# Router logits taken from rows ahead of the first norm, and expert loads issued earlier, in a two-block kernel

## The chip, the cores and the metric

One core of one Trainium2 chip runs the whole program. The metric is the device time of one execution in microseconds (us). The kernel before was run three times.

## The reference

Two transformer-like blocks on 256 tokens of width 1024, all in fp32. The part of the first block that matters here, cut to its core:

```python
merged = sigmoid(gate_a) * y_conv + sigmoid(gate_b) * y_gla
mix = merged @ w_out + b_out
x = layer_norm(ALPHA * x + mix, ln1_g, ln1_b)
ffn = hier_moe(x, w_rg, b_rg, w_re, b_re, w1, w3, w2)
x = layer_norm(ALPHA * x + ffn, ln2_g, ln2_b)
...
def hier_moe(x, ...):
    g_logits = x @ w_rg + b_rg               # 8 groups
    e_all = (x @ w_re + b_re)                # 64 experts, 8 per group
    # one group per token, the two best experts in it, softmax weights
    ...
    hdn = silu(xb @ w1[e]) * (xb @ w3[e])
    out += slot_weight * (hdn @ w2[e])
```

`w1`, `w3` (1024x512) and `w2` (512x1024) of all 64 experts are 403 MB. The second block (four mixers and a gated feed-forward part) follows.

## The kernel before, in words

Every engine has its own program, written out by hand, and they meet through semaphores. `Banks` (L128) hands out the eight PSUM banks in turn; `take` waits until a bank's last reader is done. `Line.done` (L203) makes an engine wait for its own last operation.

**End of the first block's mixers** (`block1_pe`, `block1_dve`, `block1_act`, `block1_sp`). TensorE computes the conv output in eight tiles (`co0` to `co7`, L363). VectorE gates each (`gate_conv`, L971) and adds the other branch into the merged tile (L973), in buffer 8 of `shared`. Then comes the projection: for each half `t` of the 256 rows and each half `s` of the 1024 columns, eight matmuls of 512 columns (L687; each fp32 matmul shows as two instructions). VectorE adds the residual (L1009), takes statistics (L1010, L1015), centres (L1016), inverts the deviation that ScalarE took (L819, L1019) and scales (L1020). Only then does TensorE turn the 128 rows by eight transposes (`turn_rows`, L397, its matmuls at L403), ScalarE copies them out (L826), and TensorE computes the logits (L707, bias L708). `keep_clocked` (L369, L373) is filler work for TensorE.

**The router** (`moe_dve`, from L1397) works on VectorE: the group, the two experts (`chosen`), their weights, their places. Its last reduction is L1437. VectorE then enters its loops and waits for the semaphore `round_moved`, which ScalarE gives. It builds the selection matrices of the first four experts (L1449), TensorE picks rows with them (L1207), and the expert matmuls follow (L1234 for `w1` and `w3`, L1255 for `w2`, L1261 to add up).

**The expert weights** arrive in 96 slabs of 4 MB, six for each group of four experts: two of `w1`, two of `w3`, two of `w2`. There are four slots (`PLACES`, L1106), and slab 1 of the first group goes to four spare buffers in quarters (`load_extra`, L1546). SyncE issues all loads in one order (`moe_sp`, L1519). A load waits for the semaphore `moe_read` of its slot, which TensorE gives when it has read the slab before. The first loads wait for what lay in those buffers: slot 0 is free when the input split is over, slot 1 holds weights of the conv output, slot 2 (`PLACES` 0) holds `w_out`, slot 3 (`PLACES` 6) holds the merged tiles. Once four slots are full, the next load can go only when TensorE has read the first slab.

```python
for i in (2, 3):
    pe.drain().then_inc(S(f"moe_read{i}"), FREED)
...
load(0, 0, 0, True)
for n in (0, 1):
    load_extra(n)
load(2, 0, 0, True)
load_extra(2)
for i in (3, 4):
    load(i, 0, 0, True)
for t in range(TT):
    K.banks1.wait_full(sp, f"logits{t}")
load_extra(3)
```

Of the kernel before, what the change touches and what calls it, by code (L numbers as in the profile page):

```python
# [23 lines left out]
P = 128  # L24
T = 256
TT = T // P
# [39 lines left out]
                 hg_g=2, pool_s=2, n_mem=8, n_mix_pre=8)  # L66
# [330 lines left out]
def turn_rows(K, pe, banks, name, rows, t):  # L397

    for half in range(2):
# [131 lines left out]
def block1_pe(K, pe):  # L531
# [146 lines left out]
    pe.drain().then_inc(S("moe_read1"), FREED)  # L678
    m8 = K.tiles(8, DT)
    for t in range(TT):  # L680
        for s in range(2):
            w = K.slab(R.wait_landed(pe, f"wo{s}"))
            b = B.take(pe, f"wo{t}_{s}")
            for j in range(DT):
                if s == t == 0:
                    pe.wait_ge(S("merged1"), j + 1)
                ins = pe.matmul(K.psum[:, b, :], m8[:, j, t * P:(t + 1) * P], w[:, j, :], start=(j == 0),  # L687
                                stop=(j == DT - 1))
            ins.then_inc(B.full[b], 1)
            if t == TT - 1:  # L690
                R.last_group[f"wo{s}"] = f"wo1_{s}"
    for i in (2, 3):
        pe.drain().then_inc(S(f"moe_read{i}"), FREED)

    V = moe_views(K)
    pe.wait_ge(S("router_in"), 32)
    for t in range(TT):
        if t:
            keep_clocked(K, pe, B, "clocked0", 1)
        pe.wait_ge(S("x1"), t + 1)  # L700
        turn_rows(K, pe, B, "turn_x", K.tiles(1, TT, D), t)
        b = B.take(pe, f"logits{t}")
        o = K.psum[:, b, 0:NG + NE]
        for k in range(DT):
            if k % 4 == 0:
                B.wait_read(pe, f"turn_x{t}_{k // 4}")
            pe.matmul(o, V.x[:, k, t * P:(t + 1) * P], V.w_router[:, k, :], start=(k == 0), stop=False)  # L707
        pe.matmul(o, K.con[32:33, CON["ones"][0]:CON["ones"][0] + P], K.A(5, NG + NE, 1610)[32:33, :], start=False, stop=True)\  # L708
          .then_inc(B.full[b], 1)


def block1_act(K, act):
# [107 lines left out]

    row_sd(0)
    for t in range(TT):
        for half in range(2 - t):
            g = f"turn_x{t}_{half}"
            B.wait_full(act, g)
            L.read(act.activation(x1[:, 4 * half:4 * half + 4, t * P:(t + 1) * P], turned(K, B, "turn_x", t, half),  # L826
                                  ACT.Copy), B, g)
        if t == 0:
            row_sd(1)
        b = B.wait_full(act, f"logits{t}")  # L830
        L.read(act.activation(router_views(K).logits[:, t, :], ps[:, b, 0:NG + NE], ACT.Copy), B, f"logits{t}")
# [3 lines left out]
def block1_dve(K, dve):  # L835
# [124 lines left out]
    ga, gb = K.tiles(8, DT), K.tiles(9, DT)  # L960
# [6 lines left out]
    def gate_conv(m):  # L967
# [5 lines left out]
        L.done(dve.tensor_tensor(ga[:, m, :], ga[:, m, :], gb[:, m, :], ALU.add), S("merged1"))  # L973
# [13 lines left out]
    mem, mem_rstd = K.tiles(10, DT), K.A(5, T, 1756)  # L987
    for m in range(DT):
        gate_conv(m)
        if m == 0:  # L990
# [21 lines left out]
    for t in range(TT):  # L1012
        for s in range(2):
            add_out(t, s)
        L.done(dve.bn_aggr(K.stat("mean_var", 2 * t, 2), K.stat("bn", 12 * t, 12)), S("ln1_stats"))  # L1015
        L.done(dve.scalar_tensor_tensor(x1[:, t, :], x1[:, t, :], K.stat("mean_var", 2 * t), K.gain("ln1_g"),  # L1016
                                        ALU.subtract, ALU.mult), S("dve_steps"))
        dve.wait_ge(S("row_sd"), ROW_SD["ln1"] + t + 1)
        L.done(dve.reciprocal(K.stat("rstd", t), K.stat("sd", t)), S("dve_steps"))  # L1019
        L.done(dve.scalar_tensor_tensor(x1[:, t, :], x1[:, t, :], K.stat("rstd", t), K.gain("ln1_b"),  # L1020
                                        ALU.mult, ALU.add), S("x1"))
    g = f"turn_x{TT - 1}_1"
    B.wait_full(dve, g)
# [82 lines left out]
PLACES = (4, 2, 0, 6)  # L1106
# [75 lines left out]
def moe_pe(K, pe):  # L1182
# [14 lines left out]
    def quad(pair, half, first=False):  # L1197
# [3 lines left out]
        pe.wait_ge(S("total_added"), n * 4 + 1)  # L1201
# [95 lines left out]
def moe_act(K, act):  # L1297
# [10 lines left out]
    L.done(act.activation(K.A(2), K.A(1), ACT.Copy, scale=ALPHA1), S("total_added"))  # L1308
# [23 lines left out]
    act.sem_inc(S("round_moved"), 1)  # L1332
# [10 lines left out]
    act.wait_ge(S("total_added"), rounds * (NQ * 4) + 1)  # L1343
# [19 lines left out]
def router_views(K):  # L1363
    class W:
# [16 lines left out]
        count = K.A(5, 1, 1602)  # L1381
    return W
# [8 lines left out]
def moe_dve(K, dve):  # L1391
# [8 lines left out]
    for t in range(TT):  # L1400
        B.wait_read(dve, f"logits{t}")
# [19 lines left out]
    dve.sem_inc(S("chosen"), 1)  # L1421

# [1358 lines left out]
```

## Time and profile before

| what | value |
|---|---|
| median of 3 runs | 1707.75 us (1706.77 to 1707.82) |
| profiled execution, its own time | 1708.29 us |
| its span | 1706.4 us |
| TensorE busy | 1378.0 us, 81% |
| VectorE busy | 650.5 us, 38% |
| ScalarE busy | 445.5 us, 26% |
| read from HBM | 528.79 MB, 310 GB/s over the span |
| TensorE clock, mean | 0.915 of full |

The span is from the first to the last instruction of the profiled execution. Busy time is not a bound by itself: an engine can be busy while another sets the pace. Times inside the trace are counted from the start of the span.

### The profile page before, as it was taken

To read this page: it belongs to the slowest core of one execution; us is meant where nothing else is said; L and a number is where in the kernel's file an instruction comes from. 1 tells how busy PE (TensorE), PEld (TensorE's weight loads), DVE (VectorE), ACT (ScalarE), POOL (GpSimd) and SP (SyncE) were. 2 spreads that over 40 slices of the span, in tenths; PEclk is the share of its full clock that TensorE was granted. 3 is DMA by queue.
4 is the path that set the end of the run, shared out by engine and by line. 5 is a ranking of instruction groups with operands and counts; after the bars stand their busy time and mean duration, and the time that the engine had idled before them with its cause. 6 is when DMAs were issued, how large, how long until landed. Compare 5 with 4: busy or idle time off the path is not lost.

```text
span 1706.4 us, 20849 instructions
## 1 busy us (share of the span) xinstructions
PE 1378.0 (81%) x8454; PEld 882.1 (52%) x8454; DVE 650.5 (38%) x1076; ACT 445.5 (26%) x645; POOL 0.7 (0%) x6
## 2 busy tenths in 40 slices
PE   8999999877566656666676666566799999999998
PEld 7889986522122212212221222122399989778887
DVE  5887954311011101110110011011266888655874
ACT  4454230201001001000010010010263764456653
POOL 0000000000000000000000000000000000000000
PEclk9999999998788888988887878787899999999999
DMA  8433347799999999999999999999944324565540
GB/s 348 158 136 142 143 157 311 308 425 431 431 429 436 432 432 431 430 431 432 434 432 433 431 430 431 430 433 434 409 180 148 119 80 174 197 240 178 188 173 26
DMA packets 50440, 530.76 MB, mean 311 GB/s; under 512 B 4276, under 2 KB 5556, under 8 KB 33862
## 3 DMA queue, kind: packets, MB, share of 16 engines
q1 hardware_dynamic: 50374, 529.86, 75.0%
q8 instruction: 45, 0.74, 0.2%
q14 instruction: 21, 0.17, 0.0%
HBM read 528.79 MB, written 1.05 MB: 310 GB/s over the span
## 4 chain that ended last, share of the span: by engine, by line
PE 55%; DMA 40%; DVE 2%; ACT 1%; issue 1%; SPq 0%; DVEq 0%; ACTq 0%
DMA ring<-in_w 35%; PE psum L363 9%; PE psum L445 6%; PE psum L446 6%; PE psum L447 6%; PE psum L1234 5%; PE psum L1987 4%; PE psum L1255 4%; DMA shared<-in_w 4%; PE psum L1988 2%; PE psum L1261 2%; PE psum L687 2%; PE psum L1207 1%; PE psum L1824 1%; DMA arena<-in_w 1%; PE psum L549 1%
## 5 line engine op out<-in xcount | busy, mean ns | idle before, releaser
L1234 PE MATMUL psum<-shared,arena 128*32 128x512 f32 x1008 | 148.1, 737 | 78.5 <-DMA shared<-in_w 78.4
L1234 PE MATMUL psum<-ring,arena 128*32 128x512 f32 x1024 | 144.1, 716 | 69.9 <-DMA ring<-in_w 69.8
L1464 DVE TENSOR_TENSOR shared<-shared,psum 128x512 f32<-128x512 f32 x16 | 11.0, 686 | 461.6 <-PE psum L1234 461.6
L1234 PEld LDWEIGHTS psum<-shared,arena 128*32 128x32 f32 x1008 | 35.5, 131 | 181.4 <-DMA shared<-in_w 96.1
L445 PE MATMUL psum<-parts 128*128 128x256 f32 (+1 forms) x392 | 128.0, 327 | 0.0
L1255 PE MATMUL psum<-ring,shared 128*32 128x512 f32 x512 | 81.6, 784 | 56.8 <-DMA ring<-in_w 56.8
L447 PE MATMUL psum<-parts 128*128 128x256 f32 (+1 forms) x392 | 126.8, 323 | 0.0
L446 PE MATMUL psum<-parts 128*128 128x256 f32 (+1 forms) x392 | 126.7, 323 | 0.0
L1255 PE MATMUL psum<-shared 128*32 128x512 f32 x512 | 81.6, 784 | 53.4 <-DMA shared<-in_w 52.7
L1234 PEld LDWEIGHTS psum<-ring,arena 128*32 128x32 f32 x1024 | 35.9, 128 | 171.3 <-issue 91.4
L1987 PE MATMUL psum<-parts 128*128 128x512 f32 x308 | 110.5, 398 | 1.3 <-DVEq L2545 1.3
L1466 DVE COPY shared<-psum 128x512 f32<-128x512 f32 x16 | 11.1, 691 | 249.8 <-PE psum L1255 249.8
L1713 DVE TENSOR_TENSOR parts<-ring,parts 128x1024 fp32r<-128x1024 f32 x66 | 80.9, 1225 | 56.4 <-ACT parts L1706 54.1
L864 DVE SCALAR_TENSOR_TENSOR arena<-arena,vec 128x256 f32<-128x256 f32 x240 | 98.7, 479 | 2.0
L445 PE MATMUL psum<-parts,ring_parts 128*128 128x256 f32 x336 | 96.0, 286 | 1.3 <-DVE ring_parts L1661 0.7
L446 PE MATMUL psum<-rowbuf_parts,ring_parts 128*128 128x256 f32 x336 | 94.6, 282 | 0.0
L447 PE MATMUL psum<-parts,ring_parts 128*128 128x256 f32 x336 | 93.9, 279 | 0.0
L1988 PE MATMUL psum<-parts 128*128 128x256 f32 x352 | 91.6, 281 | 0.0
L1706 ACT ACTIVATE parts<-ring 128x1024 fp32r<-128x1024 f32 x66 | 70.0, 1061 | 74.0 <-PE psum L1989 41.1
L1326 ACT ACTIVATE arena<-psum 128x256 f32<-128x256 f32 x16 | 6.1, 383 | 316.9 <-PE psum L1244 316.9
L1207 PE MATMUL psum<-arena 128*128 128x128 f32 x512 | 65.2, 288 | 27.4 <-DVE arena L1449 27.4
L1330 ACT ACTIVATE shared<-psum 128x512 f32<-128x512 f32 x16 | 9.6, 597 | 295.0 <-PE psum L1255 295.0
(304 smaller groups left out, 2264.1 us busy)
## 6 DMA issues: line engine op xcount, KB each, us to landing
shared<-in_w SPq DMA_DIRECT2D x47, 4096.0 KB, 32.3
ring<-in_w SPq DMA_DIRECT2D x47, 4096.0 KB, 32.5
ring<-in_w_in SPq DMA_DIRECT2D x19, 2048.0 KB, 8.5
ring<-in_w_ffn_gate_up SPq DMA_DIRECT2D x11, 2048.0 KB, 8.5
ring<-in_w_gate SPq DMA_DIRECT2D x8, 2048.0 KB, 7.8
ring<-in_w_ffn_down SPq DMA_DIRECT2D x5, 2048.0 KB, 7.7
ring<-in_w_out SPq DMA_DIRECT2D x4, 2048.0 KB, 7.6
ring<-in_w_gla_out SPq DMA_DIRECT2D x2, 2048.0 KB, 7.6
```

The lines of the kernel that those rows point to most:

```text
L363: m = pe.matmul(o, weights[k], acts[k], start=(k == 0), stop=(k == n - 1 and bias is None))
L445: pe.matmul(out, w[0], x[0], start=start, stop=False)
L446: pe.matmul(out, w[0], x[1], start=False, stop=False)
L447: return pe.matmul(out, w[1], x[0], start=False, stop=stop)
L864: ins = dve.scalar_tensor_tensor(conv[:, m, :], u[:, m, w:w + T], cw[:, m, w:w + 1], conv[:, m, :], ALU.mult, ALU.add)
L1207: m = pe.matmul(ps[:, bank, k % 4 * P:(k % 4 + 1) * P], V.x_rows[:, t, k * P:(k + 1) * P], V.sel[:, t, :], start=(t == 0), stop=(t == TT - 1))
L1234: m = pe.matmul(ps[slots, bank, :], V.picked[:, k, slots], w[e * len(w) // QUAD][:, e % (QUAD // len(w)), j, :], start=(k == 0), stop=(k = ...
L1255: m = pe.matmul(ps[slots, MOE_BANK["down"][c], :], V.hidden_t[:, f, slots], w(e), start=(f == 0), stop=(f == ET - 1))
L1706: L.done(L.eng.activation(self.shaped(n, 0), src, ACT.Copy), K.sem("unit_high"))
L1713: L.done(L.eng.tensor_tensor(self.shaped(n, 1), src, self.shaped(n, 0).bitcast(F32), ALU.subtract), K.sem("unit_low"))
L1987: pe.matmul(ps[:, b, :], w[0][:, k, :], sp.both[:, k, :, :], start=(k == 0), stop=False)
L1988: m = pe.matmul(ps[:, b, 0:T], w[1][:, k, :], sp.u[0][:, k, :], start=False, stop=False)
```

## The change

It moves and adds work, and computes the same thing.

The logits are taken from the rows before the norm. With x the row before the norm, m its mean and r its inverse deviation, the logits of the normed row are r (x @ (g w)) - r m (sum of g w) + (sum of b w + bias). So VectorE scales the router's weights by the gain and takes two column sums (`router_sums`) while the conv output is computed. TensorE spreads them over the partitions by two small matmuls (`router_const`), and turns the rows before the norm and computes their logits between the matmuls of the projection. VectorE scales and shifts the result (`logit_shift`, `logits`). The scaling of the second 128 rows stands in the router, behind `chosen`.

The merged tiles go to buffer 2, which the total of the experts uses later. ScalarE writes that total when both halves of the rows are ready, under a semaphore `total_ready` of its own. VectorE gives `round_moved` itself for the first round. Slots 2 and 3 change places (`PLACES`), the slot of the merged tiles being free when they have been added. Load 0 and the quarters 0 and 1 go behind `co0`, load 3 behind the last merged tile.

```diff
+def ps_cols(K, b, n):
+    return K.psum[:, b, 0:n]
@@ block1_pe
-    pe.drain().then_inc(S("moe_read1"), FREED)
-    m8 = K.tiles(8, DT)
-    for t in range(TT):
-        for s in range(2):
...
-    for i in (2, 3):
-        pe.drain().then_inc(S(f"moe_read{i}"), FREED)
...
+    for i in (1, 2):
+        pe.drain().then_inc(S(f"moe_read{i}"), FREED)
+    W = router_views(K)
+    ones_row = K.con[32:33, CON["ones"][0]:CON["ones"][0] + P]
+    pe.wait_ge(S("router_sums"), 2)
+    b = B.take(pe, "router_const")
+    pe.matmul(ps_cols(K, b, 2 * (NG + NE)), K.c("ones"), W.column_sums, start=True, stop=False)
...
+    def turn(t, half):
+        B.wait_read(pe, f"wo{t}_{half}")
+        turn_rows(K, pe, B, "turn_x", rows, t, (half,))
+    def logits(t, half):
+        group = f"logits{t}"
+        b = B.place[group][0] if half else B.take(pe, group)
+        B.wait_read(pe, f"turn_x{t}_{half}")
+        for k in range(4 * half, 4 * half + 4):
+            m = pe.matmul(ps_cols(K, b, NG + NE), V.x[:, k, t * P:(t + 1) * P], V.w_router[:, k, :], start=(k == 0),
+                          stop=(k == DT - 1))
+        if half:
+            m.then_inc(B.full[b], 1)
+    project(0, 0)
+    project(0, 1)
+    turn(0, 0)
+    project(1, 0)
+    turn(0, 1)
+    project(1, 1, 0, 4)
+    turn(1, 0)
+    logits(0, 0)
+    logits(0, 1)
+    project(1, 1, 4, DT)
+    pe.drain().then_inc(S("moe_read3"), FREED)
+    logits(1, 0)
+    turn(1, 1)
+    logits(1, 1)
@@ block1_dve
+    def router_sums(name, scaled, out):
+        gain = last(K.v(name, 0, DT), NG + NE)
+        L.done(dve.tensor_tensor(scaled, V.w_router, gain, ALU.mult), S("dve_steps"))
+        L.done(dve.tensor_reduce(out, scaled.rearrange("p k n -> p n k"), AX, ALU.add), S("router_sums"))
...
+    add_out(0, 0)
+    add_out(0, 1)
+    gathered(0)
+    logit_shift(0)
+    add_out(1, 0)
+    centred(0)
+    scaled_rows(K, L, 0)
+    logits(0)
+    add_out(1, 1)
+    gathered(1)
+    centred(1)
+    logit_shift(1)
+    logits(1)
@@ block1_sp
-    for slab in SLABS1[-4:]:
+    load("co0")
+    moe_load(K, sp, 0, 0, 0, True)
+    for n in (0, 1):
+        moe_load_extra(K, sp, n)
+    for slab in ("co1", "wo0"):
         load(slab)
...
+    load("wo1")
@@
-PLACES = (4, 2, 0, 6)
+PLACES = (4, 2, 6, 0)
@@ moe_act
-    L.done(act.activation(K.A(2), K.A(1), ACT.Copy, scale=ALPHA1), S("total_added"))
+    act.wait_ge(S("x1"), TT)
+    L.done(act.activation(K.A(2), K.A(1), ACT.Copy, scale=ALPHA1), S("total_ready"))
...
-    act.sem_inc(S("round_moved"), 1)
@@ moe_dve
     dve.sem_inc(S("chosen"), 1)
+    scaled_rows(K, L, 1)
...
+        dve.wait_ge(S("total_ready"), 1)
...
+    dve.sem_inc(S("round_moved"), 1)
@@ moe_sp
-    load(0, 0, 0, True)
-    for n in (0, 1):
-        load_extra(n)
     load(2, 0, 0, True)
-    load_extra(2)
+    moe_load_extra(K, sp, 2)
+    sp.wait_ge(S("merged1"), DT)
     for i in (3, 4):
         load(i, 0, 0, True)
```

SyncE, from the first load of the conv output's weights to the last load ahead of the experts' loop, before (`in_w` is the experts' weights, `bank_full` a finished PSUM group; the name in front of `<-` is the buffer written):

```order
L1057 DMA ring<-in_w_conv_out 128x4096 [waits bank_full2]
L1057 DMA ring<-in_w_conv_out 128x4096 [waits bank_full6]
...
L1057 DMA ring<-in_w_out 128x4096 [waits bank_full0]
L1074 DMA arena<-in_x_rows 128x2x1024 [waits bank_full6]
L323 DMA arena<-in_gains 128x1024 [waits conv_act]
...
L1537 DMA shared<-in_w 128x8192 [waits moe_read0]
L1549 DMA rowbuf<-in_w 128x2048
L1549 DMA shared<-in_w 128x2048
L1537 DMA ring<-in_w 128x8192 [waits moe_read1]
...
L1537 DMA ring<-in_w 128x8192 [waits moe_read2]
L1537 DMA shared<-in_w 128x8192 [waits moe_read3]
L1549 DMA arena<-in_w 128x2048 [waits bank_full4,bank_full0]
```

And the same stretch of SyncE in the changed kernel:

```order
L1130 DMA ring<-in_w_conv_out 128x4096 [waits bank_full2]
L1615 DMA shared<-in_w 128x8192 [waits moe_read0]
L1628 DMA rowbuf<-in_w 128x2048
L1628 DMA shared<-in_w 128x2048
L1130 DMA ring<-in_w_conv_out 128x4096 [waits bank_full6]
...
L1130 DMA ring<-in_w_out 128x4096 [waits bank_full0]
...
L1615 DMA ring<-in_w 128x8192 [waits moe_read1]
L1628 DMA shared<-in_w 128x2048
L1615 DMA shared<-in_w 128x8192 [waits merged1,moe_read2]
L1615 DMA ring<-in_w 128x8192 [waits moe_read3]
L1628 DMA arena<-in_w 128x2048 [waits bank_full3,bank_full2]
```

The load into slot 0 and two quarters moved ahead of the second slab of the conv output's weights. The load into slot 2 now waits for the last merged tile instead of the end of the projection.

TensorE, from the last two groups of the projection to the logits, before:

```order
L687 MATMUL psum<-ring,shared 128x512 [waits bank_free5,ring1_landed1]
L687 MATMUL psum<-ring,shared 128x512 x7
L403 MATMUL psum<-con,arena 128x128 [waits bank_free6,x1,router_in]
L403 MATMUL psum<-con,arena 128x128 x3
L403 MATMUL psum<-con,arena 128x128 [waits bank_free7]
...
L707 MATMUL psum<-shared,arena 128x72 [waits bank_free6,bank_free0]
L707 MATMUL psum<-shared,arena 128x72 x3
...
L708 MATMUL psum<-shared,con 128x72
```

And in the changed kernel, from the first half of the last group (L703 is the projection, L408 the turn, L719 the logits):

```order
L703 MATMUL psum<-ring,arena 128x512 [waits bank_free0,ring1_landed1]
L703 MATMUL psum<-ring,arena 128x512 x3
L408 MATMUL psum<-con,arena 128x128 [waits bank_free1,bank_free6]
...
L719 MATMUL psum<-shared,arena 128x72 [waits bank_free5,bank_free2]
...
L719 MATMUL psum<-shared,arena 128x72 [waits bank_free7]
...
L703 MATMUL psum<-ring,arena 128x512 [waits ring1_landed1]
L703 MATMUL psum<-ring,arena 128x512 x3
L719 MATMUL psum<-shared,arena 128x72 [waits bank_free1,bank_free3]
...
L408 MATMUL psum<-con,arena 128x128 [waits bank_free4,bank_free0]
...
L719 MATMUL psum<-shared,arena 128x72 [waits bank_free4]
```

Before, the turns and logits stand behind the whole projection and wait for the normed rows (`x1`). Now three of the four turns and the first logits stand within it, and only half a turn and the second logits behind it.

VectorE, in the router, from `chosen` to the start of its loops, in the changed kernel:

```order
L1481 TENSOR_SCALAR shared<-shared 128x128 [waits dve_steps]
L1096 SCALAR_TENSOR_TENSOR arena<-arena,stats 128x1024 [waits dve_steps]
L1479 TENSOR_TENSOR shared<-shared 128x128 [waits expert_exp,x1]
...
L1520 TENSOR_REDUCE shared<-psum 128x1 [waits bank_full0,bank_free7]
L1559 UNCONDITIONAL_BRANCH [waits bank_free0]
L1560 UNCONDITIONAL_BRANCH
L1560 ISA
L1532 ISA [waits round_moved]
L1532 TENSOR_TENSOR arena<-con,shared 128x128
```

The row at L1096, the scaling of 128 rows of 1024, is new in this place; the rest stands as before.

## Rows read from the trace of the kernel before

**Rows 1.** The page: chain by line, and GB/s in 40 equal slices.

```profile
DMA ring<-in_w 35%; PE psum L363 9%; PE psum L445 6%; PE psum L446 6%; PE psum L447 6%; PE psum L1234 5%; PE psum L1987 4%; PE psum L1255 4%; DMA shared<-in_w 4%; PE psum L1988 2%; PE psum L1261 2%; PE psum L687 2%; PE psum L1207 1%; PE psum L1824 1%; DMA arena<-in_w 1%; PE psum L549 1%
...
GB/s 348 158 136 142 143 157 311 308 425 431 431 429 436 432 432 431 430 431 432 434 432 433 431 430 431 430 433 434 409 180 148 119 80 174 197 240 178 188 173 26
```

**Rows 2.** Windows: length, PE, PEld, DVE, ACT, POOL busy, clock, DMA share, GB/s.

```profile
292.00:307.00 15.00, 15.00 (x36) 6.46 (x34) 5.71 (x8) 0.29 (x1) 0.00 (x0) 1.00 0.08 34
...
331.00:332.00 1.00, 0.77 (x7) 0.58 (x6) 0.00 (x0) 0.20 (x1) 0.00 (x0) 1.00 0.12 49
...
346.00:1210.00 864.00, 564.89 (x3570) 192.13 (x3570) 87.01 (x165) 59.83 (x90) 0.00 (x0) 0.84 1.00 431
```

**Rows 3.** Timeline of SyncE's queue: start, length, line, operation, count.

```profile
252.18 0.40 SPq L1537 DMA_DIRECT2D shared<-in_w  x1
...
279.53 0.33 SPq L1537 DMA_DIRECT2D ring<-in_w  x1
...
307.50 0.33 SPq L1537 DMA_DIRECT2D ring<-in_w  x1
...
331.07 0.35 SPq L1537 DMA_DIRECT2D shared<-in_w  x1
341.06 3.80 SPq L1537 DMA_DIRECT2D ring<-in_w  x2
```

**Rows 4.** Timeline of TensorE, 279 to 334 us: start, busy, line, idle before.

```profile
279.65 27.70 PE L687 MATMUL psum<-ring,shared 128*128 128x512 f32 x64 [0.26 <-issue]
307.73 1.07 PE L403 MATMUL psum<-con,arena 128*128 128x128 f32 x8 [0.38 <-issue]
309.20 1.98 PE L707 MATMUL psum<-shared,arena 128*128 128x72 f32 x16 [0.40 <-ACT arena L826]
311.11 0.44 PE L708 MATMUL psum<-shared,con 1*128 1x72 f32 x2
...
324.19 2.92 PE L1207 MATMUL psum<-arena 128*128 128x128 f32 x24 [2.31 <-DVE arena L1449]
327.04 3.64 PE L1234 MATMUL psum<-shared,arena 128*32 128x512 f32 x32
...
333.39 0.59 PE L1234 MATMUL psum<-rowbuf,arena 128*32 128x512 f32 x1 [1.62 <-DMA arena<-in_w]
```

**Rows 5.** Timeline of VectorE and ScalarE, 306 to 326 us.

```profile
310.69 1.28 DVE L1020 SCALAR_TENSOR_TENSOR arena<-arena,stats 128x1024 f32<-128x1024 f32 x1
...
313.16 0.60 ACT L826 ACTIVATE arena<-psum 128x512 f32<-128x512 f32 x1 [1.29 <-PE psum L403]
...
316.70 0.17 DVE L1398 TENSOR_REDUCE shared<-shared 128x2 f32<-128x16 f32 x1 [2.41 <-ACT shared L831]
...
319.96 0.23 DVE L1397 TENSOR_SCALAR shared<-shared 128x128 f32<-128x128 f32 x1
...
322.23 0.22 DVE L1437 TENSOR_REDUCE shared<-psum 128x1 f32<-128x64 f32 x1
...
323.44 0.49 DVE L1449 TENSOR_TENSOR arena<-con,shared 128x128 f32<-128x128 f32 x2 [0.99 <-ACTq L1332]
```

**Rows 6.** Chain that ended last, in order of time: start, length, what.

```profile
185.91 93.48 PE psum L363 x432
...
316.32 16.93 DMA arena<-in_w
```

**Rows 7.** Groups of VectorE, 255 to 281 us: busy, mean ns, idle before.

```profile
L971 DVE SCALAR_TENSOR_TENSOR shared<-psum,vec,shared 128x256 f32<-128x256 f32 x8 | 3.9, 483 | 16.3 <-PE psum L363 16.3
```

**Rows 8.** DMA issues from 279 to 280 us: KB, us from issue to landing.

```profile
ring<-in_w SPq DMA_DIRECT2D x1, 4096.0 KB, 11.9
```

**Rows 9.** DMA issues from 331 to 332 us.

```profile
shared<-in_w SPq DMA_DIRECT2D x1, 4096.0 KB, 15.3
```

**Rows 10.** DMA queues from 345 to 520 us: packets, MB, share of 16 engines.

```profile
q8 instruction: 6, 0.10, 0.2%
```

**Rows 11.** Timeline of TensorE, 1190 to 1213 us.

```profile
1202.09 5.34 PE L1234 MATMUL psum<-shared,arena 128*32 128x512 f32 x32 [4.08 <-DMA shared<-in_w]
```

More of the change, by code:

```diff
@@ L394, in pe_mean_by_tile, with turn_rows @@
     m.then_inc(banks.full[b], 1)
-def turn_rows(K, pe, banks, name, rows, t):
-    for half in range(2):
+def turn_rows(K, pe, banks, name, rows, t, halves=(0, 1)):
+    for half in halves:
         b = banks.take(pe, f"{name}{t}_{half}")
@@ new lines, in block1_pe, with project @@
+    W = router_views(K)
[3 more added lines that the diff above has]
+    pe.matmul(ps_cols(K, b, 2 * (NG + NE)), K.c("ones"), W.column_sums, start=True, stop=False)
+    pe.matmul(K.psum[:, b, NG + NE:2 * (NG + NE)], ones_row, K.A(5, NG + NE, 1610)[32:33, :], start=False, stop=True)\
+      .then_inc(B.full[b], 1)
+    m8, V, rows = K.tiles(2, DT), moe_views(K), K.tiles(1, TT, D)
+    def project(t, s, k0=0, k1=DT):
+        w = K.slab(R.wait_landed(pe, f"wo{s}"))
+        group = f"wo{t}_{s}"
+        b = B.take(pe, group) if k0 == 0 else B.place[group][0]
+        for j in range(k0, k1):
+            if s == t == 0:
+                pe.wait_ge(S("merged1"), j + 1)
+            ins = pe.matmul(K.psum[:, b, :], m8[:, j, t * P:(t + 1) * P], w[:, j, :], start=(j == 0), stop=(j == DT - 1))
+        if k1 == DT:
+            ins.then_inc(B.full[b], 1)
+        R.last_group[f"wo{s}"] = group
@@ L819, in row_sd, with turned_rows @@
         L.done(act.activation(K.stat("sd", t), K.stat("mean_var", 2 * t + 1), ACT.Sqrt, bias=K.c("ln_eps")), S("row_sd"))
+    def turned_rows(t, half):
+        g = f"turn_x{t}_{half}"
+        B.wait_full(act, g)
+        L.read(act.activation(x1[:, 4 * half:4 * half + 4, t * P:(t + 1) * P], turned(K, B, "turn_x", t, half), ACT.Copy),
+               B, g)
     row_sd(0)
     for t in range(TT):
[L823 to L831, printed above, removed]
+        for half in range(2):
+            turned_rows(t, half)
+    row_sd(1)
     act.preload_act_table(ACT.Exp)
@@ L1200, in quad @@
         pe.wait_ge(S("sel_built"), n * 4 + 2)
-        pe.wait_ge(S("total_added"), n * 4 + 1)
+        if first and half == 0:
+            pe.wait_ge(S("x1"), TT)
+        else:
+            pe.wait_ge(S("total_added"), n * 4)
         def pick(a, b):
@@ new lines, in moe_load @@
+def moe_load(K, sp, i, first, pair, start=False, final=False):
+    S, d, ring = K.sem, K.d, MoeRing(K)
+    t = ring.turn(i, start)
+    i %= PAIR * len(SLABS3)
+    name, cut = SLABS3[i % len(SLABS3)]
+    sp.wait_ge(ring.passed(t), pair * USES + t // RSLABS + FREED)
+    sp.sem_inc(S("set_wanted"), 1)
+    dst = ring.slab(t, 1).rearrange("p e k n -> p k (e n)")
+    src = d[name].rearrange("s p n -> p s n")[:, bass.ds(first + (i // len(SLABS3) * CUTS + cut), 1), :]
+    if not final:
+        sp.dma_start(dst, src).then_inc(ring.landed(t), 16)
+        if (name, cut) == SLABS3[-1]:
+            for piece in (1, 2, 3):
+                sp.sem_inc(S(f"w2_piece{piece}"), 16)
+        return
+    for piece in range(4):
+        h = slice(SLAB_COLS // 4 * piece, SLAB_COLS // 4 * piece + SLAB_COLS // 4)
+        sp.dma_start(dst[:, :, h], src[:, :, h]).then_inc(S(f"w2_piece{piece}") if piece else ring.landed(t), 16)
@@ L1560, in moe_sp @@
         K.banks1.wait_full(sp, f"logits{t}")
[L1561 removed]
+    moe_load_extra(K, sp, 3)
     sp.wait_ge(S("rounds_known"), 1)
@@ L2319, in inverse_sums @@
             B.wait_read(dve, f"{name}{AH - 1}")
-        L.done(dve.reciprocal(V.sums, V.sums), S("sums"))
+        L.done(dve.reciprocal(V.sums, V.sums), step)
     def shares(name):
```

108 lines of the change are left out of this document (41 added, 67 removed).

## The prediction

> **What bounds the kernel now.** I read the page first: the row of bytes per slice and the chain of waits [rows 1]. From slice 9 to slice 28 the core moves 430 GB/s without a break, and 35% of the chain that ended last is the expert weights landing in `ring`. The windows say the same of one stretch: from 346 to 1210 us the 16 DMA engines are at share 1.00 and 431 GB/s, with TensorE busy 565 of 864 us [rows 2]. That is 9.7 us for a 4 MB slab (4.194 MB / 431 GB/s). There are 96 slabs, so the middle of the kernel is one stream, and its end is where it starts plus its length. No instruction of the change alters the bytes. So the question is what sets the start of the stream, and whether all of its bytes must be moved after that.
>
> Next the queue of SyncE [rows 3]. I call the loads #0, #2, #3, #4 (4 MB each) and e0 to e3 (the quarters of slab 1). Before, #0 and e0, e1 go at 252 us, #2 with e2 at 279.5, #3 and #4 at 307.5, e3 at 316.3 [rows 6] and #5 at 331.07. From 292 to 307 the DMA engines stand at share 0.08, so 15 us are idle there; from 331 to 332 they stand at 0.12 [rows 2]. Then #5 starts the stream. #5 goes into the slot of #0 and is issued when TensorE has read #0: its 32 matmuls run from 327.04 for 3.64 us, to 330.7 [rows 4]. Whatever is loaded earlier, #5 waits for this. **The start of the stream hangs on the chain projection, norm, router, first selection, first slab, and not on the loads before it.**
>
> Third, that chain [rows 4, 5]. The projection runs 279.65 to 307.35. The router's first operation on VectorE is at 316.70, 9.35 us later. Its last reduction ends at 322.45, VectorE then waits 0.99 us for a semaphore of ScalarE, the selection starts at 323.44, the first pick at 324.19, the first slab at 327.04.
>
> **The change, part by part.** *#0, e0 and e1 go at 200 us instead of 252.* They are 6.3 MB, 14.6 us at 431 GB/s. Behind them on SyncE stand `co1`, `wo0`, the rows of x, `wo1` and two gains. `co1` waits for its slot until about 214 anyway, and is read only in the second half of the conv output, which runs to 279.4. TensorE runs one unbroken piece from 185.9 to 279.4 [rows 6], so nothing there waits for a load. Cost nothing. If that cover went, each load would be late by at most 14.6 us less its slack of tens of us.
>
> *Column sums on VectorE.* Four operations on 576 elements at the second and third tile of the conv output. The trace has none of this size; the nearest are 1.28 us for 1024 columns [rows 5] and 0.48 for 256 [rows 7], so they cost 2 to 5.1 us together. I take 2.8, by size. The eight operations at L971 waited 16.3 us in all for TensorE [rows 7], and the two gaps used are about 2 us each. Hidden. If it were not, the last merged tile would be late, and the projection asks for that one only at its eighth matmul.
>
> *TensorE gets work before the end of the projection.* The constant: one matmul of 144 columns and one on one partition, at most 0.44 us for such a pair [rows 4], 0.6 together. Three turns of 4 transposes, half of the 1.07 us that 8 take [rows 4]: 1.6. The logits of the first 128 rows: 1.9 (16 instructions from 309.20 to 311.11) [rows 4]. Sum 4.1, all on the path, since the projection is unbroken. It ends at 307.35 + 4.1 = 311.45.
>
> *The chain behind it is shorter.* Before 9.35 us. Now: 0.38 until TensorE starts again (307.35 to 307.73), 0.95 for half of the logits, 0.53 for the last turn, 0.2 to ScalarE, 0.60 for its copy [rows 5], 0.14, 0.95 for the other half, then 0.1 and 0.24 for the scaled sum on VectorE: 4.1. Beside it VectorE has the centring (1.28), a reciprocal and two small operations behind the last turn, which ends about 0.15 later; I take 4.25. The router starts at 315.7, 1.0 us earlier.
>
> *Behind the router.* One 1024-column operation (1.28, with its gap 1.32) [rows 5] now stands between `chosen` (320.19) and the weights, ahead of everything that leads to the selection: 1.32 later. The wait of 0.99 us for ScalarE goes, since VectorE now gives that semaphore itself. What takes its place is VectorE's own way into its loop, which the trace hides under that wait: between 0 and 0.99, I take 0.5, the middle. Net: 1.0 - 1.32 + 0.99 - 0.5 = 0.2 us earlier for the selection, for the first slab and for #5. The bounds are 0.7 earlier and 0.3 later, and 1 us more on either side for the inserted TensorE work.
>
> *#3 goes at 280.5 and #4 at about 312.* #2, e2 and #3 are 9.4 MB, done by 304; #4 and e3 are done by about 326 instead of 333.25 (316.32 + 16.93, the end of e3 in the chain) [rows 6]. So the idle stretch moves: it was 292 to 307, now it is some 8 us before 312 and some 6 us from 326 to 332. The 4 MB brought forward do not shorten the stream, because #5 is not ready to follow. This is why a load moved by 27 us is worth almost nothing by itself.
>
> *What a queue that has run empty is worth.* TensorE waited 1.62 us for e3 [rows 4]; that goes, and #6 (issued at 341.06) [rows 3] goes about 1 us earlier. #5 needed about 1 us from issue to its bytes (331.07 to 332) and 9.7 us of transfer, so it left the engines at 341.7 while #6 could start at 342.1: 0.4 us regained. By mean bytes the sum is therefore 0.2 + 0.4 = 0.6 us. But a slab counts when its last part has landed. #2, issued into an empty queue, landed after 11.9 us [rows 8]. #5, issued behind e3, landed after 15.3 [rows 9]. Some of the 16 engines were behind by 3.4 us, and at a constant pace this lag stays to the end of the stream. After the change #5 finds the queue empty, as #2 did: 0.2 + 3.4 = 3.6 us.
>
> The Trainium skill, DMA: Bandwidth & Descriptors, section Why a DMA increments its semaphore by 16 and not by 1, says that a transfer runs "on up to 16 SDMA engines that finish independently, and the semaphore counts them". By that rule the sum would be 3.6, by the mean bytes of the windows 0.6; the 15.3 beside 11.9 us agrees with the rule.
>
> Between 0.6 and 3.6 I choose by the instruction packets. From 345 to 520 us six of them take 0.2% of 16 engines [rows 10], 0.2% x 16 x 175 / 6 = 0.9 us of one engine each. An engine hit twice is 1.9 us behind, and becomes the new slowest one: 3.6 - 1.9 = 1.7 us. Behind the stream nothing changes. The profiled execution took 1708.29 us (span 1706.4), so it should take 1706.6. The median of the runs, 1707.75, is 0.5 below it: **forecast 1706.0**, from 1707.75 - 1.7 = 1706.05.
>
> **The rivals.** What can be told from no change is 0.2%, 3.4 us.
> A. The forecast, 1706.0, chance 0.52.
> B. No gain from the lag: instruction packets or the start-up leave one engine as late as before, or the inserted work costs 1 us more. Gain 0.6 down to a loss of 1.3: 1707.2 to 1709.1. For it speaks that six such packets fall into the 175 us behind the start of the stream [rows 10]. Chance 0.28.
> C. The lag goes entirely and the chain is at its best bound: 3.4 + 0.7 = 4.1, 1703.6. Against it: the packets. Chance 0.12.
> D. The 9.7 us of #3 come off the whole: 1698.0. For it: 15 idle us of DMA. Against it: #5 waits for the read of #0. Only if the first slab could be read 9 us sooner. Chance 0.03.
> E. Slower: TensorE's clock. Before, TensorE stood idle 2.31 us before the first pick and kept full speed (32 matmuls in 3.64) [rows 4]. After an idle 4.08 us late in the stream the same 32 took 5.34 [rows 11]. Now its filler work ends earlier and the selection hardly does, so the idle is about 2.8 us. If the clock falls to its lower level (1.2 of 2.4 GHz), the pick (2.92) and the slab (3.64) double, #5 goes 6.5 us later, and with the 1.7 gained the time is 1707.75 + 4.8 = 1712.5. It decides somewhere between 2.31 and 4.08 us of idle. Chance 0.05.
>
> The Trainium skill, TensorE: Matmul & The Clock Gate, section Part 1: The HAM clock gate, says that "the default state is throttled, and activity releases the throttle"; the 5.34 beside 3.64 us agrees, and it is the rule by which E would come.
>
> **How the numbers follow.** The likeliest case gives 1706.0. The range, 1703.6 to 1709.2, takes in A, B and most of C, and leaves out D, E and the far edge of C, about 1 in 10. Faster by over 0.2%: C and D, 0.15. Slower: E, 0.05. Within: 0.80.
>
> **What would show each step.** #5 issued between 330.0 and 331.5 us. The projection's last matmul at 311 to 312. The DMA share near zero for some us just before #5, and full from there to about 1208. #5 landing 11.9 to 13 us after its issue. The first TensorE wait for e3 gone. No wait of VectorE between 185 and 280 that holds TensorE. I am wrong if #5 goes more than 1.5 us away from 331, if TensorE's granted clock is below 1.00 between 320 and 335, or if the stream's length from #5 to its end changes by more than 3.6 us.

## The result, and the profile after

| | before | after |
|---|---|---|
| median | 1707.37 us (1705.91 to 1708.74, 15 runs) | 1710.03 us (1707.96 to 1712.07, 15 runs) |
| profiled execution, its own time | 1708.29 | 1710.75 |
| its span | 1706.4 | 1709.0 |

The ratio is 1.0014, 95% interval 1.0008 to 1.0021: the change made the kernel 0.14% slower, 2.7 us. That is less than the 0.2% that I called the bound of what can be told, but the interval excludes no change, and 1710.0 is outside my range of 1703.6 to 1709.2. The spans differ by 2.6 us, so the two traces hold the loss. Of all executions of this document one was slow: one of the eleven of `b_vec16` (experiment 1) took 1898.59 us at a mean granted clock of 0.72, and the ratios leave it out.

**Up to the first pick the trace does what I said.** SyncE after, its last loads:

```profile
200.34 0.35 SPq L1615 DMA_DIRECT2D shared<-in_w  x1
...
280.41 0.33 SPq L1615 DMA_DIRECT2D shared<-in_w  x1
311.41 0.33 SPq L1615 DMA_DIRECT2D ring<-in_w  x1
315.02 0.33 SPq L1628 DMA_DIRECT2D arena<-in_w  x1
333.25 0.35 SPq L1615 DMA_DIRECT2D shared<-in_w  x1
```

VectorE after:

```profile
315.61 0.17 DVE L1482 TENSOR_REDUCE shared<-shared 128x2 f32<-128x16 f32 x1
...
319.27 1.28 DVE L1096 SCALAR_TENSOR_TENSOR arena<-arena,stats 128x1024 f32<-128x1024 f32 x1 [0.15 <-DVE shared L1481]
...
322.48 0.22 DVE L1520 TENSOR_REDUCE shared<-psum 128x1 f32<-128x64 f32 x1
323.28 0.49 DVE L1532 TENSOR_TENSOR arena<-con,shared 128x128 f32<-128x128 f32 x2 [0.58 <-DVEq L1558]
```

The projection's last piece starts at 307.63 and lasts 3.65, so it ends at 311.28 (forecast 311.45). The router starts at 315.61 (315.7), and the selection at 323.28: 0.16 us earlier than in [rows 5], where I had worked out 0.2. VectorE's way into its loop took 0.58, where I took 0.5. The four operations for the column sums took 3.9 us together, where I took 2.8, and no wait of TensorE between 185 and 280 us answers to them.

**The first pick.** TensorE after, the rows that answer to [rows 4]:

```profile
307.63 3.65 PE L703 MATMUL psum<-ring,arena 128*128 128x512 f32 x8
...
324.03 5.26 PE L1288 MATMUL psum<-arena 128*128 128x128 f32 x24 [3.47 <-DVE arena L1532]
329.21 3.64 PE L1315 MATMUL psum<-shared,arena 128*32 128x512 f32 x32
...
334.63 0.62 PE L1315 MATMUL psum<-rowbuf,arena 128*32 128x512 f32 x1 [0.69 <-ACT arena L1400]
```

The 24 matmuls of the pick took 5.26 us instead of 2.92 [rows 4], after an idle 3.47 instead of 2.31. The windows say why (from 320 to 327 us; the columns are those of [rows 2]). Before:

```profile
320.00:327.00 7.00, 4.43 (x36) 3.95 (x34) 3.74 (x14) 3.38 (x4) 0.49 (x2) 1.00 1.02 437
```

After:

```profile
320.00:327.00 7.00, 3.53 (x19) 3.42 (x19) 3.41 (x13) 3.49 (x4) 0.49 (x2) 0.65 0.72 305
```

The granted clock fell from 1.00 to 0.65, a mean over both of its levels: it was 1.00 up to 321 us, 0.69 from 321 to 324, so it fell while TensorE was still idle, and 0.50 from 324 to 328. The slab behind the pick ran its 3.64 us at full speed again. So the fall cost 2.34 us, and #5 went 2.18 us later than in [rows 3], at 333.25. The wait for `e3` of 1.62 us [rows 4] is gone, as predicted.

**The stream took that back.** Windows after:

```profile
292.00:307.00 15.00, 15.00 (x53) 7.79 (x51) 6.22 (x10) 2.09 (x4) 0.00 (x0) 1.00 0.74 316
308.00:331.00 23.00, 18.14 (x100) 13.56 (x102) 11.74 (x40) 7.16 (x13) 0.49 (x2) 0.85 0.57 229
331.00:332.00 1.00, 1.00 (x16) 0.35 (x12) 0.00 (x0) 0.00 (x0) 0.00 (x0) 1.00 0.00 0
346.00:1210.00 864.00, 561.95 (x3574) 189.07 (x3574) 87.36 (x166) 60.39 (x91) 0.00 (x0) 0.85 1.00 432
```

The idle stretch of the DMA engines has moved from 292 to 307 us [rows 2] to the time before #5, and #5 finds its queue empty (DMA share 0.00 from 331 to 332). DMA issues after, the row of #5, from 333 to 334 us:

```profile
shared<-in_w SPq DMA_DIRECT2D x1, 4096.0 KB, 13.5
```

It landed after 13.5 us, not 15.3 [rows 9]. To measure the stream I take a mark in the second block that every build has, 64 matmuls in 13.81 us (I call it the mark). It stands first in each of the next two fences.

**The loss is behind the stream.** The chain of waits in order of time: start, length, what. Before:

```profile
1242.36 13.81 PE psum L1747 x64
1273.13 1.78 PE psum L1787 x16
1286.22 1.78 PE psum L1787 x16
...
1380.92 2.03 PE psum L1902 x24
```

After:

```profile
1241.86 13.81 PE psum L1830 x64
1272.94 1.79 PE psum L1870 x16
1286.24 1.79 PE psum L1870 x16
...
1382.13 2.03 PE psum L1985 x24
```

From #5's issue to the mark it was 911.29 us before (1242.36 - 331.07), and is 908.61 now: 2.68 shorter. So the mark is 0.50 earlier (1241.86 against 1242.36). From the mark to the end of the span it was 464.04 (1706.4 - 1242.36), and is 467.14: 3.10 longer, in a part of the program that the change does not touch. This adds up: -0.16 (selection) + 2.34 (clock) - 2.68 (stream) + 3.10 = 2.6.

What is longer there? Between the mark's end and the first row of 16 stand 144 matmuls of `three_passes`. They took 1273.13 - 1256.17 = 16.96 us before, 117.8 ns each, and 1272.94 - 1255.67 = 17.27 now, 119.9 ns each. One in three of them, the second of each triple, reads `rowbuf_parts`. Groups of TensorE from 1255 us to the end, before:

```profile
L445 PE MATMUL psum<-parts,ring_parts 128*128 128x256 f32 x336 | 96.0, 286 | 1.3 <-DVE ring_parts L1661 0.7 <-ACT shared L2021 0.6
L446 PE MATMUL psum<-rowbuf_parts,ring_parts 128*128 128x256 f32 x336 | 94.6, 282 | 0.0
L447 PE MATMUL psum<-parts,ring_parts 128*128 128x256 f32 x336 | 93.9, 279 | 0.0
```

After:

```profile
L450 PE MATMUL psum<-parts,ring_parts 128*128 128x256 f32 x336 | 97.2, 289 | 0.7 <-DVE ring_parts L1744 0.4 <-ACT shared L2104 0.2
L451 PE MATMUL psum<-rowbuf_parts,ring_parts 128*128 128x256 f32 x336 | 95.4, 284 | 0.0
L452 PE MATMUL psum<-parts,ring_parts 128*128 128x256 f32 x336 | 95.4, 284 | 0.0
```

Some 1000 such matmuls at 2.1 ns more make about 2.1 us. The rest is one place. The chain after, at 1378 us:

```profile
1378.02 0.58 PE psum L450
1378.60 0.22 PE psum L451
1378.82 0.21 PE psum L452
...
1380.32 0.15 PE psum L450
1380.46 0.12 PE psum L451
```

Most of the matmuls there stand at 0.21 us instead of 0.12. The ten from 1378.02 on take 2.44 us to the end of the tenth; before, the same ten took 1.45 (1377.83 to 1379.28). Windows before and after, the same stretch:

```profile
1377.80:1380.30 2.50, 2.47 (x21) 2.48 (x21) 1.06 (x1) 2.34 (x6) 0.00 (x0) 1.00 0.00 0
```

```profile
1377.80:1380.30 2.50, 2.30 (x12) 2.28 (x11) 1.23 (x2) 2.34 (x6) 0.00 (x0) 0.51 0.00 0
```

The granted clock is 0.51 there, about its lower level (1.2 of 2.4 GHz). It costs 1.0 us, and 2.1 + 1.0 makes the 3.10.

### The profile page after: what moved, and what is told of

Same layout as the page of the kernel before. It is cut to its first block, busy times and chain, and to the rows that moved or that the text cites. A ratio compares the mean times of both kernels' runs of the same rounds, so it can differ in the third digit from the quotient of the medians.

```text
span 1709.0 us, 20845 instructions
## 1 busy us (share of the span) xinstructions
PE 1378.2 (81%) x8452; PEld 883.3 (52%) x8452; DVE 656.0 (38%) x1086; ACT 445.8 (26%) x644; POOL 0.7 (0%) x6
## 4 chain that ended last, share of the span: by engine, by line
PE 57%; DMA 38%; DVE 3%; ACT 1%; issue 1%; DVEq 0%; SPq 0%; ACTq 0%
DMA shared<-in_w 37%; PE psum L363 9%; PE psum L450 6%; PE psum L1315 6%; PE psum L451 6%; PE psum L452 6%; PE psum L2070 4%; PE psum L1336 4%; PE psum L2071 2%; PE psum L1342 2%; PE psum L1288 2%; PE psum L703 2%; PE psum L1907 1%; PE psum L554 1%; PE psum L2041 1%
## 5 line engine op out<-in xcount | busy, mean ns | idle before, releaser
L1336 PE MATMUL psum<-shared 128*32 128x512 f32 x512 | 89.4, 834 | 68.5 <-DMA shared<-in_w 68.5
L1336 PE MATMUL psum<-ring,shared 128*32 128x512 f32 x512 | 75.5, 743 | 44.3 <-DMA ring<-in_w 43.6
```

Source lines behind the costliest of these rows:

```text
L1336: m = pe.matmul(ps[slots, MOE_BANK["down"][c], :], V.hidden_t[:, f, slots], w(e), start=(f == 0), stop=(f == ET - 1))
```

## The experiments

My theories after the traces. **Place:** the change adds sixteen columns (eight of gain and eight of bias of the first norm) to the constant buffer `vec`, 64 bytes per partition, and every buffer declared behind it moves by 64 bytes; `rowbuf_parts` is one, and the matmuls of `three_passes`, which work with it, became slower. **Clock:** the longer idle before the first pick costs 2.3 us. Rivals: the second block is slower in some executions whatever the place; the early loads themselves are what costs.

The experiments ran in three jobs; the kernel before ran in each (medians 1707.6, 1707.05, 1707.94 us).

**1. `b_vec16`: the kernel before, with the 16 columns and nothing else.**

```diff
-                 hg_g=2, pool_s=2, n_mem=8, n_mix_pre=8)
+                 hg_g=2, pool_s=2, n_mem=8, n_mix_pre=8, ln1_gain=8, ln1_shift=8)
```

> The kernel before, with the 16 further columns in the vector table and nothing else; they push the buffer `rowbuf` (read as `rowbuf_parts` by the three-pass matmuls of the second block) 64 bytes further. Theory of the address: those 1056 matmuls go from 117.8 to about 120 ns each, so the time rises by 2.0 to 3.1 us over before, all of it between 1255 and 1490 us of the span. Rival, the loss comes from the moved router and loads: no change within 0.7 us.

1708.89 us, ratio 1.0008 (0.9999 to 1.0017). From the mark to the end 466.10 us (before 464.04), 144 matmuls in 17.28. So the slower pace comes with the columns, without any other part of the change. The whole, 1.3 us above the kernel before of its job, is less than the 2.0 to 3.1 that I expected, and its interval just reaches no change: the stream was shorter here, to which "Read together" below returns.

**2. `a_tail`: the changed kernel, the 16 columns in a buffer of their own behind all others.**

```diff
-        self.vec = sb("vec", NVEC)
+        self.vec = sb("vec", NVEC - TAIL)
...
+        self.vec_tail = sb("vec_tail", TAIL)
```

> The changed kernel, with its 16 columns in a small buffer behind all others, so that every other buffer lies where it lay before. Theory of the address: 2.0 to 3.1 us less than the changed kernel, so about 1707.3, equal to before; the second block is back at its old length. Rival: no different from the changed kernel, 1710.0. Either way the first pick is still slow (24 matmuls in 5.3 us), since the addresses do not touch it.

1707.84 us, ratio 1.0004 (0.9995 to 1.0013). This removes 2.2 us of the loss (1710.03 - 1707.84), as expected. From the mark to the end it is 464.29, 2.85 less than in the changed kernel: the 144 matmuls are back at 16.96 us, and the fall of the clock at 1378 us is also absent from this trace (granted clock 1.00 from 1373 to 1381).

**3. `a_clk`: the changed kernel, six more filler matmuls before the first pick.**

```diff
+    for _ in range(6):
+        pe.matmul(ps[:, 5, 0:T], K.c("ident"), K.con[:, CON["after"][0]:CON["after"][0] + T], start=True, stop=True)
     for g in ("before0", "before1", "chose"):
```

> The changed kernel with six filler matmuls on TensorE behind the three router matmuls, so that it idles about 0.8 us before the first pick instead of 3.47. Theory of the clock: the pick takes 2.92 instead of 5.26 us, load 5 is issued about 2.3 us sooner (331.0), and the whole kernel is 2.0 to 2.3 us shorter than the changed one, 1707.8. Rival, the stream hides it (the stretch behind load 5 gave it back): less than 0.7 us.

1708.27 us, ratio 1.0005 (0.9996 to 1.0014): 1.8 below the changed kernel, a little less than the 2.0 to 2.3 that I expected. Timeline of TensorE, the pick:

```profile
324.71 2.92 PE L1290 MATMUL psum<-arena 128*128 128x128 f32 x24 [0.83 <-DVE arena L1534]
```

It is back at 2.92 us, and it waits for the selection (L1534) as before, not for the fillers, which end at 323.89. It starts 0.7 later than in the changed kernel only because the projection already started that much later in this execution (281.15 against 280.44). #5 went at 331.59, 1.66 earlier than in the changed kernel, and the mark came 1.69 earlier.

**4. `a_tail_clk`: both edits.**

> Both edits together. If address and clock add up: 4.3 to 5.4 us less than the changed kernel, 1705.2, which is 2.2 us less than before. If they overlap: about 1707.5.

1706.35 us, ratio 0.9994 (0.9985 to 1.0003), 3.7 below the changed kernel. The two effects about add up (2.2 + 1.8 = 4.0), though it is less than the 4.3 to 5.4 that I expected. One thing in its timeline of TensorE is not as in the other builds:

```profile
312.65 1.25 PE L723 MATMUL psum<-shared,arena 128*128 128x72 f32 x8 [0.75 <-ACT arena L856]
313.69 5.68 PE L382 MATMUL psum<-con 128*128 128x256 f32 x18
```

These 18 filler matmuls took 4.10 us in the changed kernel; the granted clock is 0.50 from 314 to 316 us here, after an idle of only 0.75. They push the new fillers past the selection, so the pick starts without an idle, at 323.42, about 0.6 later than it could (selection at 322.10, and 0.75 from there to the pick in the changed kernel).

**5. `a_tail_clk_late`: the same, with load 3 held until the projection has ended**, so that loads 3 and 4 both go at 312 us.

```diff
-    sp.wait_ge(S("merged1"), DT)
+    sp.wait_ge(S("moe_read3"), FREED)
     for i in (3, 4):
```

> The kernel with both edits (columns at the end, six filler matmuls), and load 3 held back until the projection is read, so that loads 3 and 4 go together at 311 us as they did at 307.5 before. Theory of the empty queue: the queue is still busy with e3 when load 5 is issued, load 5 lands 15 us and not 13.6 us after its issue, and the kernel is 1 to 2 us slower than with load 3 at 280 us. Rival: the preloads never matter, no difference within 0.5 us.

1712.56 us, ratio 1.0031 (1.0021 to 1.0042): 6.2 above `a_tail_clk` (of another job; 6.3 by the two ratios), much more than the 1 to 2 that I expected. Its timeline shows a chain that I had not seen. SyncE:

```profile
311.67 0.33 SPq L1622 DMA_DIRECT2D shared<-in_w  x1
312.11 0.36 SPq L1622 DMA_DIRECT2D ring<-in_w  x1
315.24 0.33 SPq L1635 DMA_DIRECT2D arena<-in_w  x1
331.12 0.35 SPq L1622 DMA_DIRECT2D shared<-in_w  x1
347.97 0.34 SPq L1622 DMA_DIRECT2D ring<-in_w  x1
```

TensorE:

```profile
337.60 1.03 PE L1322 MATMUL psum<-rowbuf,arena 128*32 128x512 f32 x1 [5.79 <-DMA arena<-in_w]
```

The quarter `e3` lands behind loads 3 and 4. TensorE waits 5.79 us for it, reads slab 1 late, and #6 goes at 347.97 instead of 339.29; the engines run dry (DMA share 0.65 from 340 to 350 us, where `a_tail_clk` has 0.98). The changed order of the projection delays load 4 from 307.5 to 311.4, and the early load 3 is what pays for that.

**6. `b_clk`: the kernel before, four more filler matmuls** (the edit of 3, at the same place).

> The kernel before, with four filler matmuls (1.9 us) behind the three router matmuls, so that TensorE idles about 0.4 us and not 2.31 before the first pick. In the profile of the kernel before the clock held there, in that of the one with 16 more columns it did not, after the same idle. If the clock falls in part of the executions of before: 0.3 to 1.2 us less than before, 1706.8. If it nearly never does: no change, 1707.6. The distance to the kernel with both edits says what moving the router and the loads is worth by itself: 0 to 1.5 us.

1707.73 us, ratio 1.0002 (0.9993 to 1.0011): no gain. The pick took 2.92 us after an idle 0.54, as in the kernel before after 2.31, so there was nothing to win at the pick. In its trace the mark comes 1.65 us earlier than before (1240.71), but the clock falls behind it (0.50 from 1375 to 1377 us), and from the mark to the end it is 465.29, 1.25 longer. Against `a_tail_clk`, by the two ratios, the router and the loads are worth 1.4 us, in the range of 0 to 1.5 that I gave; the intervals overlap.

**7 to 11. Where the place matters.** Unused columns in the kernel before, each one execution with a profile, so that the times of single pieces in the trace can be compared and the whole time can't.

```diff
         self.vec = sb("vec", NVEC)
+        self.pad = sb("pad", 8)
```

`b_pad32` and `b_pad256` have 32 and 256 columns at the same place. `b_pad16_row` has 16 directly ahead of `rowbuf`, so that only `rowbuf` and the statistics behind it move. `b_pad16_end` has 16 behind `rowbuf`, so that only the statistics move.

> The kernel before with `rowbuf` 32 bytes further on, and nothing else. Look at the three-pass matmuls at L445 to L447 from 1256 us on: before one came every 117.8 ns, with 64 bytes more every 120. If what counts is the place within 64 bytes, some third value, up to 120; if only half-way steps of 128 bytes count, 117.8 as before.

> The kernel before with `rowbuf` 128 bytes further on. If the pace repeats every 128 bytes: 117.8 ns a matmul and the second block as long as before. If any shift costs: 120 ns and 2 us more.

> The kernel before, with 64 unused bytes per partition right ahead of rowbuf, so that the vector constants, wf and small stay where they were and rowbuf (with the small statistics behind it) alone is shifted. If the place of rowbuf sets the matmuls' pace: the second block is 1.5 to 3 us longer than before, the matmuls that read rowbuf_parts at 284 to 290 ns instead of 279 to 286. Rival (the shift of wf, small or the constants does it): second block within 0.5 us of before.

> The kernel before, with 64 unused bytes per partition behind rowbuf: only the statistics and two counters are shifted. If the place of rowbuf sets the pace: the second block is within 0.5 us of before, matmuls at 279 to 286 ns. Rival (statistics): 1.5 to 3 us longer.

> The kernel before, with 1024 unused bytes per partition behind the vector constants. If the pace goes by the place of rowbuf modulo some power of two up to 1024 bytes: second block within 0.5 us of before. If the place before is favourable by its distance to another buffer or by larger blocks: 0.9 to 3 us longer, as after 32, 64 and 128 bytes.

| build | `rowbuf` moved by | 144 matmuls | mark to end | the execution |
|---|---|---|---|---|
| before | 0 | 16.96 | 464.04 | 1708.29 |
| `b_pad16_end` | 0 | 16.96 | 464.23 | 1707.86 |
| `b_pad8` | 32 bytes | 17.08 | 465.00 | 1709.46 |
| `b_pad16_row` | 64 bytes | 17.27 | 466.03 | 1710.82 |
| `b_vec16` | 64 bytes | 17.28 | 466.10 | 1708.34 |
| `b_pad32` | 128 bytes | 17.26 | 465.68 | 1709.05 |
| `b_pad256` | 1024 bytes | 16.96 | 464.41 | 1707.17 |

The chain of `b_pad16_row`:

```profile
1242.97 13.81 PE psum L1748 x64
1274.05 1.79 PE psum L1788 x16
1287.35 1.79 PE psum L1788 x16
```

The place of `rowbuf` alone sets the pace; what stands ahead of it or behind it does not matter. The rival that the second block is slower in some executions whatever the place is out: over all fourteen profiled builds the 144 matmuls take 16.96 us in the eight with `rowbuf` at its old place or 1024 bytes further, 17.26 to 17.28 in the five with 64 or 128 bytes, and 17.08 in the one with 32. That 1024 bytes bring the old pace back fits a rule that goes by the place within blocks of at most 1024 bytes; one build at one such distance does not show the rule. `b_pad32` has the pace of 64 bytes in the 144 matmuls but is 0.3 to 0.4 us shorter than those two from the mark to the end; that is not explained.

Why the place matters stays open. By the starts in the chain, the steps behind the first, second and third matmul of a triple take 120, 118 and 115 ns on average before, and 120 each after. They are 120 each in all five builds with 64 or 128 bytes. In the eight at the old pace some steps are shorter, and not the same ones: the third in `a_tail_clk` (113), the first in `a_tail_clk_late` (116). So what is lost is now and then a shorter step, and it is not tied to the one matmul of the three that reads the moved buffer.

**12. `a_tail_clk_l0`: as `a_tail_clk`, load 0 and the quarters 0 and 1 at their old place** (252 us instead of 200).

```diff
     load("co0")
-    moe_load(K, sp, 0, 0, 0, True)
-    for n in (0, 1):
-        moe_load_extra(K, sp, n)
```

> The changed kernel with the constants at the end and the six filler matmuls, as a_tail_clk, but load 0 and the quarters 0 and 1 issued where they stood before, behind the gains, at about 252 us instead of 200. My reasoning said that their place is worth nothing, since load 3 at 280 is what the early loads give: 1706.3, within 1 us of a_tail_clk, #5 at 330 to 331. Rival (the three loads push load 2, 3 and the quarter 2 later, so that these land beside the projection's end and the stream starts with uneven engines): #5 lands 15 to 16 us after its issue, 1708 to 1712.

1705.88 us, ratio 0.9990 (0.9981 to 0.9999), #5 at 330.11, landing 13.6 us later. Moving these three loads earlier gives nothing. This build has the lowest median of all, 2.1 us below the kernel before of its job, and is the only one whose interval excludes no change on the faster side, by 0.01%. So neither the early load 3 (experiment 5) nor these three are what costs.

**Read together: the stream and the clock.** Timeline and DMA issues of all fourteen builds:

| builds | idle, pick | #5 issued | lands after | #5 to the mark |
|---|---|---|---|---|
| before, `b_pad8`, `b_pad32`, `b_pad16_row`, `b_pad16_end` | 2.3, 2.92 | 330.8 to 331.7 | 13.9 to 15.3 | 910.9 to 911.4 |
| `b_clk` | 0.54, 2.92 | 330.92 | 14.8 | 909.8 |
| `b_vec16`, `b_pad256` | 2.3, 4.54 and 4.14 | 332.06, 332.53 | 13.6, 13.5 | 908.3, 908.4 |
| after, `a_tail` | 3.47, 5.26 and 5.13 | 333.25, 332.03 | 13.5, 13.6 | 908.6, 909.1 |
| `a_clk`, `a_tail_clk`, `a_tail_clk_l0` | 0.8 (none in `a_tail_clk`), 2.8 to 2.9 | 330.1 to 331.6 | 13.6 | 908.3 to 908.6 |
| `a_tail_clk_late` | 0.82, 2.92 | 331.12 | 16.1 | 915.4 |

Two things are seen. Wherever #5 landed within 13.6 us of its issue, the stretch to the mark was 908.3 to 909.1; where it was issued behind an `e3` that was still arriving, it was 1 to 3 us longer. The first kind also has an earlier #6: 9.05 to 9.07 us after #5 in those seven builds, 9.75 to 10.03 in the six behind `e3`, where TensorE waits 1.40 to 1.67 us for `e3`. The empty queue and the earlier #6 always came together, so these runs do not tell which of them shortens the stream. And in two builds of the kernel before the clock fell after an idle of only 2.3 us. It delayed #5 by a good microsecond, but cost nothing: the later #5 found an empty queue, and the mark was no later (1240.40 and 1240.89, before 1242.36). In its trace this is why `b_vec16` lost less than its slower pace: from #5 to the mark it is 2.95 us shorter than before, with #5 only 0.99 later. In the changed kernel the queue is empty anyway, so the fall costs its price (the 1.69 at the mark in `a_clk`).

## Why the prediction was wrong, point by point

**The step that failed** is the sentence "Behind the stream nothing changes." It rests on the order of instructions, which indeed does not change there. The term that I put at nothing measured 3.10 us (467.14 against 464.04). Sixteen new columns in a constant buffer move `rowbuf` by 64 bytes, and the matmuls of `three_passes` then start every 119.9 instead of 117.8 ns: 2.1 us. My diff left these columns out, and no rival speaks of addresses. Experiments 1, 2 and 7 to 11 show this cause. The other 1.0 us behind the stream is the clock at 1378 us. Such a fall, somewhere from 1371 to 1385 us, is in six of the fourteen profiled builds, in after and in all five with more fillers, and not in before. In all six the stretch from the mark to the end is about 1 us longer than in the builds with the same pace and no fall (465.06 to 465.29 against 464.04 to 464.41; 466.93 and 467.14 against 466.03 and 466.10). I have no cause for it: after an idle of 2.05 us (before), 1.95 (`b_vec16`) and 1.95 (after) the clock held in the first two and fell in the third. It stays open, and with it whether this term belongs to the change at all.

**Rival E, to which I gave 0.05, happened in its first half.** The idle was 3.47 us, not my 2.8, and the clock fell. I had doubled the pick and the slab, 6.5 us; only the pick slowed, 2.34. The estimate of the idle was too small: TensorE's last work ahead of the pick hangs on `chosen`, which came about 1.1 us earlier, and ended at 320.56 instead of 321.88 (324.03 - 3.47, and 324.19 - 2.31 from [rows 4]), while the selection came only 0.16 earlier, since the 1.28 us operation on 1024 columns stands between the two. A rival whose condition lies between two rows (2.31 held, 4.08 fell) deserved more than 0.05: with the condition at 2.8, about a third of the way. And no boundary between 2.31 and 4.08 is borne out: at the first pick the clock also fell after 2.3 us in two builds, and held after it in five. So an idle tells the odds here, not the outcome. Two of my three signs of being wrong came, #5 at 333.25 and a granted clock of 0.65; the fall alone would have been more than paid for by the 2.68 of the stream. The Trainium skill, TensorE: Matmul & The Clock Gate, section Part 1: The HAM clock gate, says that activity releases the throttle; the slab at full speed right behind the slow pick agrees.

**The chain: right.** Projection 311.28 (311.45), router 315.61 (315.7), selection 0.16 earlier (0.2). The inserted pieces moved the end of the projection as forecast: from start to start the constant took 0.79 us (I had 0.6), the three turns 0.44 each (1.3, I had 1.6) and the logits 1.74 (1.9), 3.9 in all against 4.1. The column sums on VectorE held nobody.

**The lag of the queue: right in kind, too small in size.** I put the stream at 3.4 us less 1.9 for instruction packets, 1.5 shorter. It was 2.68 shorter; #5 landed 1.8 sooner after its issue (13.5 against 15.3, just above my 11.9 to 13), and #6 went 0.93 sooner behind #5 (9.06 against 9.99), where I had put 0.4 on that. The 3.4 itself was too large for the landing: a load into an empty queue took 11.9 us for #2 in [rows 8], but 13.5 for #2 in the changed kernel and 13.4 in `b_vec16`. The deduction of 1.9 for packets was too large as well, so that two errors partly cancel. The two builds of the kernel before in which #5 came late show the same gain with no other part of the change, so it comes from the meeting of #5 and `e3`, by the queue, by the later #6, or by both.

**"A load moved by 27 us is worth almost nothing by itself": wrong for this order of work.** Experiment 5 shows 6.2 us for load 3. I asked only what the early load adds to the order before; with the projection 4 us longer, the same load must be early for `e3` to be in time. For load 0 and the quarters 0 and 1 the sentence holds (experiment 12).

**With the addresses restored and the idle filled the forecast is about met, in part by offset.** I gave a gain of 1.7. `a_tail_clk` gains 1.25 us on the before of its job (interval of the ratio up to 1.0003), `a_tail_clk_l0` 2.1. But in the trace of `a_tail_clk` the stretch from #5 to the mark is 2.97 us shorter and not 1.5, and the stretch behind it 1.02 longer and not 0. That the sum comes near 1.7 is luck as far as these two go.

## What to carry to other kernels

Compare the buffers' addresses too, not only the instructions: a constant added early in the list of buffers moves everything declared behind it, and the pace of matmuls that follow each other without a gap can depend on it. New small buffers go last. When a change shortens filler work ahead of a wait, work out the idle that is left and top the fillers up, so that the gain is not given back through the clock; then look through the whole trace for the clock, since in every build with more fillers it fell at another place. And ask of an early load not what it gains over the old order, but what would be late without it in the new one.

## What the runs showed of the hardware that was not expected

- The pace of back-to-back matmuls of 256 columns (`three_passes`) depended on where `rowbuf`, one of their operands, lies in a partition: 117.8 ns with `rowbuf` at its old place or 1024 bytes further, 118.6 at 32 bytes, 119.9 at 64 and at 128 (worked out from the 144 matmuls above).
- After an idle of 2.3 us before the first pick, TensorE's clock held in five builds and fell in two; after 3.47 it fell in both, after 0.8 us or less it held in all five (one trace of each). After 3.47 it was down before the pick began (0.50 from 321 to 324 us in `a_tail`); in `b_pad256` it was still 1.00 from 324 to 325, with the pick under way since 324.05. And in `a_tail_clk` it fell to 0.50 from 314 to 316 us, after an idle of 0.75.
- #5, a 4 MB load, landed after 13.5 or 13.6 us in the seven builds in which it met an idle queue, whatever its time of issue; behind a load still arriving it took 13.9 to 16.1, and the stretch of some 900 us to the mark was longer in all of those builds, though not in proportion: `b_pad16_end` landed it after 13.9 and needed 910.9, `b_clk` after 14.8 and needed 909.8. #2 into an idle queue took 11.9 us before and 13.5 after.
- A later issue can be free: #5 issued 1.0 and 1.5 us later, into an emptier queue, left the mark no later.
